# Delta rule in a fused transformer layer: which engine transposes the running inverse, and in what order the tiles' products stand

## What is computed

```python
def gated_delta_chunked(q, k, v, g, beta, s0):
    ...
    decay = jnp.where(tril, jnp.exp(jnp.where(tril, diff, 0.0)), 0.0)
    kb = kc * bc[..., None]
    a_mat = jnp.where(strict, jnp.einsum('nbhik,nbhjk->nbhij', kb, kc) * decay, 0.0)
    t_inv = lax.linalg.triangular_solve(eye + a_mat, jnp.broadcast_to(eye, a_mat.shape),
                                        left_side=True, lower=True)
    u = jnp.einsum('nbhij,nbhjv->nbhiv', t_inv, vc * bc[..., None])
    w = jnp.einsum('nbhij,nbhjk->nbhik', t_inv, kb * jnp.exp(gc)[..., None])
    def step(S, xs):
        q_i, k_i, u_i, w_i, g_i, dec_i = xs
        v_new = u_i - jnp.einsum('bhck,bhkv->bhcv', w_i, S)
        intra = jnp.einsum('bhik,bhjk->bhij', q_i, k_i) * dec_i
        o = (jnp.einsum('bhck,bhkv->bhcv', q_i * jnp.exp(g_i)[..., None], S)
             + jnp.einsum('bhij,bhjv->bhiv', intra, v_new))
        ...
    S, o = lax.scan(step, s0.astype(f32), (qc, kc, u, w, gc, decay))
```

## Time and profile before

| | us |
|---|---|
| median of 3 runs | 1171.54 (1170.84 to 1172.03) |
| profiled execution, own time | 1173.27 |
| its span, first to last instruction | 1171.5 |
| delta rule, first `turn_inv` to the start of the last `key_state` | 414.6 to 547.4 |
| PE busy in the span | 1029.5 (88%) |
| DVE, ACT, POOL busy | 433.0, 311.7, 164.0 |
| mean granted TensorE clock | 0.954 of 2.4 GHz |

### The profile page before, as it was taken

How to read it: one execution, slowest core, us unless ns; L and a number is a source line. 1 busy time by engine, 2 the same in 40 slices (tenths; PEclk the granted TensorE clock), 3 DMA queues, 4 the chain that set the end, 5 groups by cost and what they waited for, 6 DMA issues and landing times.

```text
span 1171.5 us, 14600 instructions
## 1 busy us (share of the span) xinstructions
PE 1029.5 (88%) x5595; PEld 562.0 (48%) x5595; DVE 433.0 (37%) x845; ACT 311.7 (27%) x619; POOL 164.0 (14%) x257
## 2 busy tenths in 40 slices
PE   4999999999998889989999999999919997797870
PEld 2444456666554679988544444444513332232220
DVE  1433036787775864645501200224460111100116
ACT  4122144566652434324310000111211111111111
POOL 0100020011000327770300000000110121101110
PEclk9999999999999999999999999999959999988995
DMA  9821152436110111300371110142535999999956
GB/s 387 346 90 46 70 183 88 190 116 216 73 72 16 42 39 41 98 8 1 109 284 72 72 72 10 63 166 85 216 103 192 396 401 422 422 424 423 423 226 269
DMA packets 43644, 204.20 MB, mean 174 GB/s; under 512 B 16736, under 2 KB 22320, under 8 KB 31536
## 3 DMA queue, kind: packets, MB, share of 16 engines
q1 hardware_dynamic: 32576, 171.92, 37.3%
q0 software_dynamic: 10416, 30.45, 7.3%
q10 hardware_dynamic: 576, 0.82, 0.2%
HBM read 191.79 MB, written 19.76 MB: 181 GB/s over the span
## 4 chain that ended last, share of the span: by engine, by line
PE 75%; DVE 11%; issue 5%; DMA 5%; ACT 2%; POOL 2%; SPq 0%; POOLq 0%; DVEq 0%; ACTq 0%
PE bank L1717 25%; PE bank L2311 11%; PE bank L1839 7%; PE bank L2332 5%; PE bank L2156 3%; PE bank L2154 3%; PE bank L1681 2%; PE bank L1998 2%; PE bank L1888 2%; DMA arena<-in_w_up 2%; PE bank L2299 1%; PE bank L2008 1%; PE bank L1732 1%; DMA arena<-in_w_blocks 1%; PE bank L1824 1%
## 5 line engine op out<-in xcount | busy, mean ns | idle before, releaser
L1717 PE MATMUL bank<-arena 128*128 128x512 f32 x672 | 292.6, 591 | 0.0
L1717 PEld LDWEIGHTS bank<-arena 128*128 128x128 f32 x672 | 125.4, 189 | 151.8 <-issue 151.8
L2311 PE MATMUL bank<-arena 128*32 128x512 f32 x1152 | 140.5, 642 | 32.1 <-issue 30.8
L1839 PE MATMUL bank<-arena 128*128 128x320 f32 x384 | 120.0, 454 | 0.0
L2311 PEld LDWEIGHTS bank<-arena 128*32 128x32 f32 x1152 | 42.4, 117 | 117.9 <-issue 117.9
L1839 PEld LDWEIGHTS bank<-arena 128*128 128x128 f32 x384 | 69.7, 192 | 35.7 <-issue 11.2
L1649 DVE TENSOR_TENSOR arena<-arena,bank 128x256 f32<-128x256 f32 x18 | 7.6, 421 | 174.6 <-ACT arena L1104 174.6
L1493 DVE TENSOR_TENSOR arena<-arena,bank 128x512 f32<-128x512 f32 x10 | 6.9, 688 | 168.1 <-PE bank L2156 168.1
L2332 PE MATMUL bank<-arena 128*32 128x512 f32 x576 | 65.8, 595 | 1.0 <-DVE arena L1642 1.0
L1026 ACT ACTIVATE arena<-bank 128x512 f32<-128x512 f32 x20 | 12.0, 598 | 145.7 <-PE bank L1717 145.7
L1104 ACT ACTIVATE arena<-bank 128x256 f32<-128x256 f32 x18 | 6.9, 385 | 164.2 <-PE bank L2311 164.2
(11 more groups left out here) (315 smaller groups left out, 1387.7 us busy)
## 6 DMA issues: line engine op xcount, KB each, us to landing
arena<-in_w_up SPq DMA_DIRECT2D x32, 2048.0 KB, 18.1
arena<-in_w_blocks SPq DMA_DIRECT2D x27, 2048.0 KB, 8.0
arena<-in_w_down SPq DMA_DIRECT2D x32, 1024.0 KB, 21.9
arena<-y_scratch SPq DMA_DIRECT2D x10, 512.0 KB, 7.3
arena<-in_bias POOLq DMA_DIRECT2D x3, 1536.0 KB, 10.7
arena<-mod_scratch POOLq DMA_DIRECT2D x8, 512.0 KB, 10.9
arena<-in_x SPq DMA_DIRECT2D x5, 512.0 KB, 7.0
gram_scratch<-arena SPq DMA_DIRECT2D x10, 256.0 KB, 2.5
```

The source lines that it names most:

```text
L1717: last = mm(bank, hT[:, k, tok0[i]:tok0[i] + P], w[:, k, :], start=(k == 0), stop=(k == KC - 1))
L1839: last = mm(banks[5 + half][:, 0:HTOK], w[:, k, :], hT[:, k, half * HTOK:(half + 1) * HTOK], start=(k == 0), stop=(k == KC - 1))
L2311: last = mm(banks[2 + e % 2][at, :], rowsT[e % 2][:, k, at], eup[expert % SLOTS_W][:, k, :], start=(k == 0), stop=(k == KC - 1))
```

## The change

At levels 1 and 2 of every pass, where the matrix that is transposed has blocks of 16x16 and 32x32, the PE transpose and the ACT copy are gone. In their place `flipped` is one VectorE instruction for each direction, STREAM_TRANSPOSE, which transposes every 32x32 block of a 128x512 buffer where it stands, from SBUF to SBUF. Level 3 keeps `turn_inv` and `inv_out`. Around this the order changes:

- DVE: the level-2 flips stand right behind each direction's `corrected(p, 1)`. The level-1 flips for tile `p + 1` stand behind `states(p - 1)`, ahead of `decay_pre(p + 2)`, and wait for `spread_out(p + 1)`. `solve(1, ...)` is cut in two: rows 1 to 7 ahead of `corrected(0, 1)`, rows 8 to 15 behind it and its flips.
- PE: `couple(p + 1, 1)` closes a pass, and `key_key(p + 2)` moves behind it to the head of the next pass. `key_query(p + 1)` moves from behind `couple(p, 2)` to ahead of it.
- SP: `solved_out(1)` waits for `decay_pre(2)` in place of `corrected(0, 1)`.
- Three semaphores of the routing step are merged into one (`chosen`), with the same meaning.

```diff
@@ sync, solved_out
                 elif p == 1:
-                    sp.wait_ge(S["sub0"], 1)
+                    sp.wait_ge(S["prep0"], dprep_at(2, "dpre"))
@@ scalar
-            def inv_out(p, n):
-                for d in range(2):
-                    act.wait_ge(S[f"turn_mm{d}"], NL * p + n)
...
+            def inv_out(p):
+                for d in range(2):
+                    act.wait_ge(S[f"turn_mm{d}"], p + 1)
+                    step(sc.activation(unit[d]["inv"], bank4(2 * d), ACT.Copy), f"inv{d}")
...
             for p in range(T):
-                inv_out(p, 1)
                 coupled(p, 1)
                 if p >= 1:
                     values_kept(p - 1)
-                inv_out(p, 2)
                 coupled(p, 2)
                 if p == 0:
                     decay_exp(2)
-                inv_out(p, 3)
+                inv_out(p)
@@ vector
             first_spread()
-            solve(1, 1, SUB)
...
+            def flipped(p, n, d):
+                U = unit[d]
+                src, dst = U["invT"][p % 2], U["inv"]
+                if n == 1:
+                    if p:
+                        dve.wait_ge(S["spread"], 2 * p + d - 1)
+                    if d == 1:
+                        src, dst = dst, src
+                        if p >= 2:
+                            dve.wait_ge(S["step_mm1"], step_at(p - 2, "vn"))
+                    elif p:
+                        dve.wait_ge(S["x_mm0"], NL * p)
+                step(v.transpose(dst.rearrange("p h c -> p (h c)"), src.rearrange("p h c -> p (h c)")), f"flip{d}")
+
             def corrected(p, n):
...
                     step(v.tensor_tensor(U["invT"][p % 2], U["invT"][p % 2], bank4(2 * d + 1), ALU.subtract), f"sub{d}")
-
+                    if n == 1:
+                        flipped(p, 2, d)
+
+            flipped(0, 1, 0)
+            flipped(0, 1, 1)
+            solve(1, 1, 8)
             for p in range(T):
                 if p >= 2:
                     residual(p - 1)
                 corrected(p, 1)
                 if p == 0:
+                    solve(1, 8, SUB)
                     decay_pre(2)
...
                 if p >= 1:
                     states(p - 1)
+                if p + 1 < T:
+                    flipped(p + 1, 1, 0)
+                    flipped(p + 1, 1, 1)
                 if 1 <= p < T - 2:
                     decay_pre(p + 2)
@@ tensor
             row_sums(2)
-            turn_inv(0, 1)
+            couple(0, 1)
             for p in range(T):
-                couple(p, 1)
+                if 2 <= p < T - 1:
+                    key_key(p + 1)
                 if p >= 2:
                     key_state(p - 1)
                 correct(p, 1)
                 if p >= 1:
                     new_values(p - 1)
-                turn_inv(p, 2)
-                couple(p, 2)
                 if 1 <= p < T - 1:
                     key_query(p + 1)
+                couple(p, 2)
...
-                turn_inv(p, 3)
+                turn_inv(p)
...
                 correct(p, 3)
-                if 1 <= p < T - 2:
-                    key_key(p + 2)
                 if p + 1 < T:
-                    turn_inv(p + 1, 1)
+                    couple(p + 1, 1)
```

More of the change, by code:

```diff
@@ L346, in build @@
             for n in ("prep_mm", "turn_mm", "x_mm", "q_mm", "step_mm", "erow", "qexp", "dexp", "prep", "msk",
-                      "xs", "inv", "sub", "step"):
+                      "xs", "inv", "sub", "step", "flip"):
                 sem(f"{n}{d}")
@@ L359, in build @@
             sem(f"h2_out{n}")
-        for n in ("chosen_ready", "dest_ready", "route_ready", "slots_ready", "rowsT_mm",
+        for n in ("chosen", "route_ready", "rowsT_mm",
                   "rowsT_ready", "hT_ready2", "weights_ready",
@@ L962, in _ @@
             row_exp(2)
-            def inv_out(p, n):
+            def inv_out(p):
                 for d in range(2):
-                    act.wait_ge(S[f"turn_mm{d}"], NL * p + n)
-                    dst = unit[d]["inv"]
-                    if d == 1 and n == 1:
-                        dst = unit[d]["invT"][p % 2]
-                        if p >= 2:
-                            act.wait_ge(S["step_mm1"], step_at(p - 2, "vn"))
-                    step(sc.activation(dst, bank4(2 * d), ACT.Copy), f"inv{d}")
+                    act.wait_ge(S[f"turn_mm{d}"], p + 1)
+                    step(sc.activation(unit[d]["inv"], bank4(2 * d), ACT.Copy), f"inv{d}")
             def coupled(p, n):
@@ L1543, in _ @@
                                      gsel.unsqueeze(3).to_broadcast([P, T, 4, 8]), ALU.mult))
-            step(v.tensor_tensor(picked, chosen[:, 0], chosen[:, 1], ALU.add), "chosen_ready")
+            step(v.tensor_tensor(picked, chosen[:, 0], chosen[:, 1], ALU.add), "chosen")
             count = banks[1][:, T * N_EXPERTS:(T + 1) * N_EXPERTS]
@@ L1573, in _ @@
                 step(v.tensor_tensor(named[:, :, n, :], reached[:, :, 0:TILES], payload[:, :, n:n + 1].to_broadcast([P, 2 * T, TILES]), ALU.mult),
-                     "dest_ready" if n else "dve_step")
+                     "chosen" if n else "dve_step")
             step(v.tensor_scalar(lists[:, L_CAP + SLOTS_W:L_CAP + N_EXPERTS], rank, float(n_big), float(NARROW - WIDE), ALU.is_lt, ALU.mult))
@@ L1583, in _ @@
             step(v.scalar_tensor_tensor(slot_f, table, -1.0, empty, ALU.add, ALU.add))
-            step(v.tensor_copy(slots, slot_f.rearrange("p (n e) -> p n e", n=2)), "slots_ready")
+            step(v.tensor_copy(slots, slot_f.rearrange("p (n e) -> p n e", n=2)), "chosen")
             barrier(dve, 3)
@@ L1971, in key_query, with turn_inv @@
                     last.then_inc(S[f"prep_mm{d}"], 1)
-            def turn_inv(p, n):
+            def turn_inv(p):
                 for d in range(2):
-                    U = unit[d]
-                    src = U["invT"][p % 2]
-                    if n == 1:
-                        if p:
-                            pe.wait_ge(S["spread"], 2 * p + d - 1)
-                        else:
-                            pe.wait_ge(S["first_spread"], d + 1)
-                        if d == 1:
-                            src = U["inv"]
-                        if p >= 1:
-                            pe.wait_ge(S[f"xs{d}"], NL * p)
-                    else:
-                        pe.wait_ge(S[f"sub{d}"], NL * p + n - 1)
+                    pe.wait_ge(S[f"sub{d}"], NL * p + 2)
                     for h in range(H_B):
-                        last = nc.tensor.transpose(banks[2 * d][:, h * P:(h + 1) * P], src[:, h], ident)
+                        last = nc.tensor.transpose(banks[2 * d][:, h * P:(h + 1) * P], unit[d]["invT"][p % 2][:, h], ident)
                     last.then_inc(S[f"turn_mm{d}"], 1)
@@ L1994, in couple @@
                     U = unit[d]
-                    pe.wait_ge(S[f"inv{d}"], NL * p + n)
+                    if n < NL:
+                        pe.wait_ge(S[f"flip{d}"], (NL - 1) * p + n)
+                    else:
+                        pe.wait_ge(S[f"inv{d}"], p + 1)
+                    if n == 1 and p >= 1:
+                        pe.wait_ge(S[f"xs{d}"], NL * p)
                     pe.wait_ge(S[f"msk{d}"], NL * p + n)
```

10 lines of the change are left out of this document (5 added, 5 removed).

## The result

| | before | after |
|---|---|---|
| median, 7 runs each | 1171.89 (1170.84 to 1175.04) | 1179.74 (1177.51 to 1182.71) |
| ratio after / before, 95% interval | | 1.0063 (1.0051 to 1.0076) |
| span of the profiled execution | 1171.5 | 1177.9 |
| `first_spread` starts | 412.15 | 412.75 |
| last `key_state` starts | 547.38 | 554.04 |

The changed kernel is slower by 0.6%. The forecast was 1178.7. The span grew by 6.4 us and the last `key_state` starts 6.66 later, so all of it lies ahead of that. 0.60 of it is there already when `first_spread` starts. Lines of after: the flips are L1446, `couple` L2006, `correct` L2016, `key_key` L1976, `row_sums` L1963, `turn_inv` L1992, `key_state` L2027, `decay_pre` L1336, `corrected` L1452, `gram_out` L1345, the products of DVE's `solve` L1366.

The account below looks back on a forecast made before the run. PE was busy nearly throughout, but the last pass waited for POOL's spreading, and the new order makes a loop of 34.2 to 34.4 us. +1.86 + 2.3 + 4.8 - 0.9 - 0.9 = +7.2: 1171.54 to 1178.7 us, range 1174 to 1184.

Parts of the forecast that it names:

- The flip at 0.70, 0.72 with its gap: Each DVE flip instruction takes 0.70 us, 0.72 with the gap to the next; ends kept at 0.55 and 1.40.
- The loop, 34.2 to 34.4 us per tile, +2.3 and +4.8: Next gram matrix waits for spreading through DVE, SP and POOL; the two steps to tiles 3 and 4 lengthen by these.
- PE's part beside DVE's: In the loop, `couple` and `key_key` run beside DVE's 7.85 us and take about as long.
- Pass 0, +1.86: `solve(1)` split around `corrected(0, 1)` and slow `key_key(2)` bring `couple(0, 3)` to 435.45 against 433.59.
- The stall: In pass 0, POOL's two masks hold two products of rows 8 to 15 of `solve(1)`: +2.1 us, between 0 and 2.4.
- The last pass, -0.9 and -0.9: Spreading to `couple(4, 1)` shortens by 0.9 us; inside the pass, level 2 saves 1.54 and 0.6 comes back.
- Sum: Pass 0, the two loop steps and the last pass's two savings together make the kernel 7.2 us slower.
- The signs: Profile checks: first spreading instructions end 34 us apart, DVE idles ahead of level-1 flips, PE idles 3 us before `couple(4, 1)`.
- Merged semaphores, `solved_out(1)`, `key_query` as cover: These parts were put at nothing; `key_query` ahead of `couple(p, 2)` covers the level-2 flips with 1.8 us.
- No stall: Rival: in pass 0 the masks miss the rows or POOL yields; 2.1 us less, 1176.6 us, chance 20%.
- Early gain that reaches POOL: Rival: tile 2 is spread up to 5.4 us earlier, so no change in the end, 1171.4 us; chance 8%.
- PE decides: Rival: spreadings of tiles 3 and 4 come before PE wants them, winning 14.5 us, 1157.0 us; chance 7%.

Follow-up runs that it names:

- e8: Changed kernel with POOL's two query scalings of the next tile moved behind that tile's spreading; 1170.81 us, 0.9993 of the kernel before.
- e3: Changed kernel with only PE's old order put back, `key_key(p + 2)` ahead of `couple(p + 1, 1)`; 1182.70 us, 1.0083 of the kernel before.
- e2: Changed kernel with level-1 flips last on DVE, behind `gram_out`, and PE's old order, `key_key` ahead of `couple`; 1174.98 us, 1.0011 of the kernel before.
- e1: Changed kernel with only the level-1 flips moved behind `decay_pre(p + 2)` on DVE; 1177.42 us, 1.0039 of the kernel before.
- e5: Changed kernel with POOL's `masks(1, 1)` held until DVE has issued the decay rows of tile 2; 1176.73 us, 1.0044 of the kernel before.
- e10: Changed kernel with late query scalings, PE's old order, and level-1 flips between decay rows and `corrected` on DVE; 1172.40 us, 1.0006 of the kernel before.
- e4: Kernel before with flips at level 2 alone, `key_query` ahead of `couple(p, 2)` and merged semaphores; 1169.92 us, 0.9971 of the kernel before.
- e6: Kernel before with POOL's two query scalings of the next tile moved behind that tile's spreading; 1168.10 us, 0.9959 of the kernel before.

## Why the prediction was right, step by step

- *The flip at 0.70, 0.72 with its gap.* Measured 0.71, and 0.75 from start to start within a pair. Right. POOL does not hold it: the flip at 462.33 took 0.71 beside POOL's spreading, that at 463.48 beside a mask.
- *The loop, 34.2 to 34.4 us per tile, +2.3 and +4.8.* (The terms themselves add up to 34.1 to 34.4, and the sum used 34.1.) Measured 34.5 and 34.3, +2.4 and +5.0 (7.94, 5.84 and 20.74 for the parts put at 7.85, 5.4 to 5.7 and 20.85). e8 shows that POOL's part is in it: 2.65 us less there took 2.6 and 2.9 off the two steps. e3 shows that PE's order does not make it, e2 that it opens when the flips stand behind the gram matrix. What the prediction called about as long, PE's part beside DVE's, was nearly deciding: e1 found it longer.
- *Pass 0, +1.86.* The second spreading instruction of tile 1 came at 437.85, against 435.79: +2.06, of which 0.60 was there already when the stage began. So +1.46. The stall was 1.2 in place of 2.1, since each product had begun some time after its mask, and `key_key(2)` began 0.8 earlier than forecast, counted from `first_spread`. From there to `turn_inv(0)` it was 3.4, as forecast (3.5), though only the second half was slow and 0.39 of it was a wait. `turn_inv(0)` was slow as well (1.80 in place of 1.04), which the forecast had not counted, and that gave 0.5 back. Without the stall the stage is 2.6 us shorter (e5): 1.2 of it the stall, the rest the half clock behind it.
- *The last pass, -0.9 and -0.9.* Into `couple(4, 1)` 0.86 in place of 1.70: -0.8, right. From there to the last `key_state` 22.10 in place of 24.02: -1.9. The difference is the half clock: `couple(4, 1)` took 2.31 in place of 3.44. This term was too small by 1.0: I had left the half clock of the row of before standing in the changed kernel, and no run tries it apart.
- *Sum.* +7.2 was forecast for the stage, and it grew by 6.06: +1.4 in pass 0, +2.4 and +5.0 in the steps, -0.8 and -1.9 in the last pass. The profiled executions differ by 6.47 (1173.27 and 1179.74), the medians by 7.85. So the mechanism and the large terms were right, and that 1178.7 came within 1.0 us of the median is in part luck: the terms were 1.1 too high, and differences outside the stage made up for it.
- *The signs.* The first spreading instructions ended at 462.24, 496.76 and 531.08, DVE stood idle for 6.3 to 8.1 us ahead of the flips of these tiles, and PE waited for the mask in pass 2, all as said. The wait ahead of `couple(4, 1)` was 2.87, just short of the 3 us that were named, and the held products took 0.89 and 0.86 in place of 1.1.
- *Merged semaphores, `solved_out(1)`, `key_query` as cover*: nothing in the trace speaks against their cost of nothing, and no run tries them apart. The spreading of tile 1 that waits for `solved_out(1)` started at 434.85, 3 us ahead of its second instruction, which waited for PE.
- *The rivals.* No stall: it was there, at 1.2 us. Early gain that reaches POOL: no, DVE's order kept it, as argued. PE decides: no, and e2 and e10 show that even with the loop open PE's spared work is not to be had while POOL's masks and DVE's queue feed it. The Trainium skill (VectorE: DVE Perf Modes, Rules for kernel authors) calls the DVE transpose the fastest for 32x32 within a bank. The trace does not bear that out for the latency: both flips take 1.46, and PE's 8 transposes with ACT's copy 1.35 to 1.54. A flip spares PE, which paid at level 2 (e4) and not at level 1.

What the prediction could have found and did not: the kernel before had 2 us of DVE held by POOL's scalings, right behind the rows that I cited for the stall, and I read that only as a price and not as something to win.

## What to carry to other kernels

Moving a step to an idle engine puts it into that engine's queue, and everything behind it there now waits for what the step waits for. Follow the queue until it comes back to where it started: if what stands behind feeds the engine that the step waits for, each turn of that loop is the time per tile, whatever the busy shares say. Ask also whether the relieved engine has a wait to fall into, since PE here often came back from idling at half clock, just where others waited for it. And look for work that nobody needs yet in front of work that somebody waits for: one moved line on POOL gained 0.4% on the kernel before (e6), where the whole change lost 0.6%.
